# The x chunks of a state-space layer: hi part of the weights times both parts of the tokens in one 512-column matmul

## The reference

```
h = rmsnorm(x, norm_g) * (1 + scale) + shift
q, k, v, z_a, xbc, z_s, dt_f, dt_b, g_a, g_s = split_cols(h @ w_in, IN_SPLITS)
xbc = jax.nn.silu(centred_conv(xbc, conv_w, conv_b))        # 5 taps along the tokens
xs, b_ssm, c_ssm = split_cols(xbc, (SSD_WIDTH, BC_WIDTH, BC_WIDTH))
y_f, s_f = ssd_scan(x4, dtf, a_f, bm, cm, s0_f)             # and one backward
y = y_f + jnp.flip(y_b, 1) + d_skip[:, None] * x4
y = y.reshape(bsz, length, SSD_WIDTH) * jax.nn.silu(z_s)
```

## Time and profile before

| | us |
|---|---|
| median of 3 runs | 2763.86 |
| lowest, highest | 2763.12, 2764.31 |
| span of the profiled execution | 2761.4 |
| TensorE busy | 2711.6 (98%) |
| VectorE busy | 1965.3 (71%) |
| ScalarE busy | 1481.9 (54%) |
| GpSimd busy | 172.1 (6%) |

### The profile page before, as it was taken

How to read it: one execution, slowest core, us unless ns; L and a number is a source line. 1 busy time by engine, 2 the same in 40 slices (tenths; PEclk the granted TensorE clock), 3 DMA queues, 4 the chain that set the end, 5 groups by cost and what they waited for, 6 DMA issues and landing times.

```text
span 2761.4 us, 39482 instructions
## 1 busy us (share of the span) xinstructions
PE 2711.6 (98%) x15824; PEld 2326.7 (84%) x15824; DVE 1965.3 (71%) x2292; ACT 1481.9 (54%) x2145; POOL 172.1 (6%) x242
## 2 busy tenths in 40 slices
...
DMA packets 175670, 627.89 MB, mean 227 GB/s; under 512 B 21028, under 2 KB 23332, under 8 KB 175104
## 3 DMA queue, kind: packets, MB, share of 16 engines
...
...
## 4 chain that ended last, share of the span: by engine, by line
PE 88%; DVE 6%; DMA 2%; ACT 2%; issue 1%; SPq 0%; DVEq 0%; POOLq 0%; POOL 0%; ACTq 0%
PE PM L490 19%; PE PM L502 19%; PE PM L491 19%; PE PM L506 7%; PE PM L495 7%; PE PM L496 7%; PE A L785 6%; DMA Zt<-in_w_mod 2%; DVE w_l L468 1%; DVE arena L567 1%; DVE X L1589 1%; PE PM L782 1%; PE A L782 1%; ACT w_h L463 1%; DMA raw<-in_w_in 1%
## 5 line engine op out<-in xcount | busy, mean ns | idle before, releaser
L468 DVE TENSOR_TENSOR w_l<-raw,w_h 128x1024 fp32r<-128x1024 f32 (+1 forms) x880 | 1058.7, 1220 | 671.3 <-ACT w_h L463 663.8
L463 ACT ACTIVATE w_h<-raw 128x1024 fp32r<-128x1024 f32 (+1 forms) x880 | 905.0, 1046 | 796.0 <-PE PM L502 558.4
L490 PE MATMUL PM<-w_h,hT_h 128*128 128x512 f32 x1408 | 563.5, 400 | 2.1 <-issue 1.8
L491 PE MATMUL PM<-w_h,hT_l 128*128 128x512 f32 x1408 | 549.2, 390 | 0.0
L495 PE MATMUL PM<-hT_h,w_h 128*128 128x256 f32 x1920 | 479.1, 287 | 3.2 <-DVE X L1589 1.7
L496 PE MATMUL PM<-hT_l,w_h 128*128 128x256 f32 x1920 | 470.3, 283 | 0.0
L490 PE MATMUL PM<-w_h,Z 128*128 128x512 f32 x1016 | 399.2, 393 | 0.9 <-issue 0.9
L491 PE MATMUL PM<-w_h,Z 128*128 128x512 f32 x1016 | 395.7, 389 | 0.0
L502 PE MATMUL PM<-w_l,hT_h 128*128 128x512 f32 x1408 | 377.3, 390 | 0.0
L495 PEld LDWEIGHTS PM<-hT_h,w_h 128*128 128x128 f32 x1920 | 367.2, 191 | 11.3 <-issue 6.9
L496 PEld LDWEIGHTS PM<-hT_l,w_h 128*128 128x128 f32 x1920 | 367.8, 192 | 2.1 <-issue 1.4
...
## 6 DMA issues: line engine op xcount, KB each, us to landing
...
raw<-in_w_ps SPq DMA_DIRECT2D x128, 512.0 KB, 4.7
...
```

The lines of the kernel that those rows point to most:

```text
L463: act.activation(w_h[:, k % RING, :, 0:n], half_raw(k, n), ACT.Copy).then_inc(hi_ready, 1)
L468: dve.tensor_tensor(w_l[:, k % RING, :, 0:n], half_raw(k, n), w_h[:, k % RING, :, 0:n].bitcast(F32), ALU.subtract).then_inc(lo_ready, 1)
L490: pe.matmul(tok_out(s), hi[:, kt, tk], wh, start=kt == 0, stop=False, skip_group_check=True)
L491: pe.matmul(tok_out(s), lo[:, kt, tk], wh, start=False, stop=False, skip_group_check=True)
```

## The change

For groups 1 to 7 of each layer the x chunk is computed in another form; group 0 and all other chunks stay.

- hT_h and hT_l become the two planes of one tensor hT. A matmul with a w_h tile streams hT[:, :, kt], 512 columns: the sum from the high part of the tokens lands in the left half of a PSUM bank, the one from the low part in the right half. w_l still meets the high part only, 256 columns, into the left half. A half then has 8 matmuls of 512 columns and 8 of 256.
- The sums take twice the PSUM. So w_in of these chunks is laid out by quarters (four contraction slices of 256 channels in one 512 KB piece): halves 0 to 3 make channel tiles 0 and 1 in the banks used before, halves 4 to 7 make tiles 2 and 3 in A[:, 2:4].
- ScalarE copies the right halves to SBUF (`copy_low`, steps 6 and 10), VectorE adds the left halves (`sum_x`, steps 6 and 9). The sum, x_sum, is in SBUF (Zt[:, 6]).
- The centre tap (`center_x`, steps 8 and 11, two instructions each) and the taps (`conv_x`, steps 10 and 12, eight each) read x_sum from SBUF instead of PSUM.
- The first bank pair is free once `sum_x(g, 0)` has read it. `x_wide` waits before half 4 for `stores` of the group before, `final_states` for `sum_x`.
- To stay within the number of semaphores, a few of the prologue's are merged.

```diff
+        def mm_wide(pe, c, i, banks):
+            k = K(c, i)
+            w = [t[:, k % RING].rearrange("p t n -> p (t n)") for t in (w_h, w_l)]
+            pe.wait_ge(hi_ready, k + 1)
+            for kk in range(4):
+                kt = 4 * (i % 4) + kk
+                for t in range(2):
+                    at = kk * 256 + t * P
+                    pe.matmul(banks[:, t, :].rearrange("p (x n) -> p x n", x=2), w[0][:, at:at + P], hT[:, :, kt],
+                              start=kt == 0, stop=False, skip_group_check=True)
+            pe.wait_ge(lo_ready, k + 1)
+            for kk in range(4):
+                kt = 4 * (i % 4) + kk
+                for t in range(2):
+                    at = kk * 256 + t * P
+                    mm = pe.matmul(banks[:, t, 0:256], w[1][:, at:at + P], hT_h[:, kt], start=False, stop=kt == KT - 1,
+                                   skip_group_check=True)
+            mm.then_inc(w_used, 1)
...
+                def copy_low(g, part):
+                    chunk_done(act, base + PH_SSD + g * 2, 4 + 4 * part)
+                    if part == 0:
+                        act.wait_ge(s_("conv_done"), L * 12 + 4 + g)
+                    banks = A[:, 2:4, :] if part else pair(0)
+                    act.activation(x_sum[:, part * 512:(part + 1) * 512]..., banks[:, :, 256:512], F.Copy).then_inc(s_("x_low_copied"), 1)
...
+                    if g:
+                        st[6] = st.get(6, []) + [lambda: copy_low(g, 0)]
+                        st[8] = st.get(8, []) + [lambda: center_x(g, 0)]
+                        st[10] = st.get(10, []) + [lambda: copy_low(g, 1)]
+                        st[11] = [lambda: center_x(g, 1)] + st.get(11, [])
...
+                def sum_x(g, part):
+                    dve.wait_ge(s_("x_low_copied"), 2 * (L * (NG - 1) + g - 1) + part + 1)
+                    banks = A[:, 2:4, :] if part else pair(0)
+                    held = x_sum[:, part * 512:(part + 1) * 512].rearrange("p (t n) -> p t n", t=2)
+                    ins = tt(held, banks[:, :, 0:256], held, ALU.add)
...
+                def conv_x(g, part):
+                    for j in (0, 1, 3, 4):
...
+                            o_ = x_tile(xc, t)[:, :, lo_:hi_]
+                            ins = dve.scalar_tensor_tensor(out=o_, in0=x_tile(x_sum, t)[:, :, lo_ + d:hi_ + d], scalar=taps(j, 4 * g + t),
+                                                           in1=o_, op0=ALU.mult, op1=ALU.add)
...
-                    st[12] = [lambda: conv_1(g)] + st.get(12, [])
-                    st[13] = [lambda: conv_2(g)] + st.get(13, [])
+                    if g:
+                        st[6] = st.get(6, []) + [lambda: sum_x(g, 0)]
+                        st[9] = st.get(9, []) + [lambda: sum_x(g, 1)]
+                        st[10] = st.get(10, []) + [lambda: conv_x(g, 0)]
+                        st[12] = [lambda: conv_x(g, 1)] + st.get(12, [])
```

More of the change, by code:

```diff
@@ L188 @@
 Z_RUN, Z_LOAD = z_tiles()
+WIDE_BLOCKS = [B_XBC + g for g in range(1, NG)]
 def raw_order():
@@ L258, in halves, with quarters @@
         return w.reshape(depth, rows // 256, 2, P, cols // N, N).transpose(0, 4, 1, 3, 2, 5).reshape(depth, cols // N, rows // 256, P, 2 * N)
+    def quarters(w):
+        depth, rows, cols = w.shape
+        return w.reshape(depth, 4, 4, P, cols // N, 2, N // 2).transpose(0, 4, 5, 1, 3, 2, 6).reshape(depth, cols // N, 8, P, 2 * N)
     given = {k: np.asarray(v) for k, v in inputs.items()}
     w_in, w_mod = given["w_in"], given["w_mod"]
-    given["w_in"] = halves(np.concatenate([w_in[:, :, :C_DT], w_in[:, :, C_GA:]], axis=2))
+    columns = np.concatenate([w_in[:, :, :C_DT], w_in[:, :, C_GA:]], axis=2)
+    given["w_in"], by_quarter = halves(columns), quarters(columns)
+    for b in WIDE_BLOCKS:
+        given["w_in"][:, b] = by_quarter[:, b]
     given["w_dt"] = w_in[:, :, C_DT:C_GA].reshape(DEPTH, 1, D_MODEL // 256, 2, P, 2 * NH).transpose(0, 1, 2, 4, 3, 5)\
@@ L324, in build @@
         decay_rows = [Zt[:, 7, :], Zt[:, 15, :]]
+        x_sum = Zt[:, 6, :]
         def CB(q):
@@ L662, in psum_sub, with x_tile @@
             return banks[:, t // 2, (t % 2) * 256:(t % 2 + 1) * 256].rearrange("p (s n) -> p s n", s=2)
+        def x_tile(held, t):
+            return held[:, t * 256:(t + 1) * 256].rearrange("p (s n) -> p s n", s=2)
         def x_banks(q):
@@ L791, in _ @@
             pe.wait_ge(s_("mod_rows_loaded"), 4 * DMA)
-            transpose(A[:, 1, 0:96], rows[0:96, 3]).then_inc(s_("mod_rows_T"), 1)
+            transpose(A[:, 1, 0:96], rows[0:96, 3]).then_inc(s_("c_T"), 1)
             end_phase(pe)
@@ L960, in final_states @@
                         pe.wait_ge(s_("st_stored"), L * NG + q)
+                    if q < NG - 1:
+                        pe.wait_ge(s_("x_summed"), L * (NG - 1) + q + 1)
                     pe.wait_ge(s_("xw_ready"), L * NG + q + 1)
@@ L980, in ssd_steps, with x_wide @@
                     return st
+                def x_wide(g, steps):
+                    c = base + PH_SSD + g * 2
+                    bank_wait(pe, 0, ub + U_SSD + g)
+                    for i in range(8):
+                        if i == 4 and g > 1:
+                            pe.wait_ge(s_("st_stored"), L * NG + g - 1)
+                        mm_wide(pe, c, i, pair(0) if i < 4 else A[:, 2:4, :])
+                        tiles_behind(K(c, i))
+                        for step in steps.get(i, ()):
+                            step()
                 def ssd_body(g, steps):
-                    halves(base + PH_SSD + g * 2, "ch", 0, ub + U_SSD + g, hT_h, hT_l, steps)
+                    if g:
+                        x_wide(g, steps)
+                    else:
+                        halves(base + PH_SSD, "ch", 0, ub + U_SSD, hT_h, hT_l, steps)
                     halves(base + PH_SSD + g * 2 + 1, "tok", 1, ub + U_SSD + g, hT_h, hT_l, steps, first=8)
```

66 lines of the change are left out of this document (49 added, 17 removed).

## The result

| | median, us | from to | runs |
|---|---|---|---|
| before | 2763.49 | 2762.69 to 2764.31 | 4 |
| changed | 2815.47 | 2813.73 to 2816.71 | 4 |

The changed kernel is slower: ratio 1.0188, 95% interval 1.0176 to 1.0200. The forecast was 2816. The profiled execution has a span of 2813.4 us, 52.0 more than before.

A forecast was written before the change was run, and what follows sets the result against it. A ScalarE-VectorE loop of 53.1 us, covered by TensorE's 53.7, was to become the bound at 57.7: +47.9 us for twelve groups and +4.4 for group 1, together +52, giving 2816 us, range 2802 to 2828.

The forecast's parts named there:

- the slack: ScalarE's wait for TensorE at the third exp: TensorE's 53.7 us covers the 53.1 us loop by 0.6 us.
- TensorE's waits: Per group after the change, TensorE waits 1.4 us for the fourth M and some 3.4 for step 13's w_l.
- group 1's 1.24 us: Lead of group 2's first w_h, taken off group 1's growth: 4.1 - 0.64 - 1.24 = +2.2 us in each layer.
- TensorE no longer holds up the exp: Third exp on ScalarE: its wait for TensorE goes once the loop is the longer, -0.59 us per group.
- pause behind conv_2: VectorE's pause between the end of the taps and the next w_l goes: -0.15 us per group.
- GpSimd: Taps with two SBUF tensors alternate with GpSimd's four instructions, +3.4 us; step 13's w_l gets 0.75 back: +2.65 per group.
- period: Time of each of groups 2 to 7: 53.70 us before, 57.7 after, +4.0 for 12 groups in two layers.
- The loop: ScalarE from step 0's w_h to step 9, then VectorE to add_y: 53.1 us round, sets group time once longer than TensorE's.
- rival 2: Loop from step 0's w_h to add_y has unseen slack, TensorE sets all: -12.0 us, 2752, faster; chance 0.07.
- Rival 3: VectorE keeps the port, GpSimd starves; add_y and final_states wait 2 to 3 us: 2800 to 2815; chance 0.74 together with forecast.
- TensorE's gain: Wide halves take 0.107 us less matmul time each: 0.86 us per group, 12.0 us over 112 halves at most.

The follow-up runs named there:

- e5: Kernel before with four more ScalarE centre instructions behind step 8's w_h of groups 1 to 7, written to an unread place: 2777.4 us, ratio 1.0052.
- e9: Changed kernel with eight useless 512-column matmuls filling TensorE's wait in step 13 of groups 1 to 7: 2806.6 us, ratio 1.0161 to the kernel before.
- e1: Changed kernel with the sums of x left in PSUM, where center_x and the taps read them: 2773.3 us, ratio 1.0035 to the kernel before.
- e7: Changed kernel with sums in PSUM, center_x(g, 0) behind step 9 and squares behind the next group's second w_h: 2753.3 us, ratio 0.9962 to the kernel before.
- e4: Kernel before with three more ScalarE copies of 128x256 behind step 8's w_h of groups 1 to 7, written to an unread place: 2764.1 us, ratio 1.0004.
- e2: Changed kernel with GpSimd's four instructions of a group cut to 4 of every 64 columns: 2765.0 us, ratio 1.0007 to the kernel before.
- e6: Changed kernel with a group's squares moved behind the next group's second w_h on ScalarE: 2807.3 us, ratio 1.0157 to the kernel before.
- e11: Changed kernel with the taps of conv_x(g, 1) on VectorE ahead of the fourth M instead of behind it: 2811.5 us, ratio 1.0177 to the kernel before.

## Why the prediction came out

The direction, the size and the mechanism were right; the slack, TensorE's waits and the place of group 1's 1.24 us were not, and their errors cancelled in the total. Per group of 2 to 7:

| term | forecast | measured | from |
|---|---|---|---|
| TensorE no longer holds up the exp | -0.59 | -1.01 + 0.39 = -0.62 | e5, e9 |
| copy_low(g, 0) | +0.48 | +0.48 | profile after |
| center_x(g, 0) | +1.00 | +0.98 | profile after |
| sum_x(g, 1) | +0.60 | +0.61 | profile after |
| pause behind conv_2 | -0.15 | -0.15 | profile after |
| GpSimd | +2.65 | 3.17 - 0.74 = +2.43 | profile after, e1 |
| period | 57.7 | 57.43 by the sum, 57.38 seen | |

- **The loop** is real: 52.69 us before (e5), and 52.69 + 0.48 + 0.98 + 0.61 - 0.15 + 2.43 = 57.04 for the changed kernel, where e9, which takes TensorE's clock out, shows 56.98. e7, where the loop is cut down, gives the forecast's rival 2: TensorE sets all.
- **The slack** was read wrongly. I took the idle time in front of one instruction of one group, 0.59, for the slack of a loop. It was 1.01; e4 paid nothing for 0.92. Six of the twelve groups show 0.80 to 0.82 at the same instruction, group 6 had spent 0.20 on a transfer before it, and the usual overlap of 0.10 was missing too: 0.91 of the 1.01 stood in the trace of before. e2 supports the 52.69: with GpSimd out of the way the same sum gives 52.69 + 0.48 + 0.98 + 0.61 - 0.15 - 0.74 = 53.87, and its period is 53.83.
- **TensorE's waits** were the step that failed. I gave its spare 4.85 us to the fourth M (1.4) and to step 13's w_l (3.4). It waits 2.45 to 2.84 for w_l and hardly ever for M. Part of this is a size: at full clock (e9) the two are 2.85 and 0.47. The other part is a step that the forecast lacks: behind 11 of the 14 waits the granted clock fell to 0.50, TensorE lost 1.6 to 2 us there (e6, and the busy time of group 6), and with them the wait for M. The earlier trace rows show a clock of 1.00 and no idle time, but the trace of before has such a fall, between the layers, and the forecast makes no use of it (the matmuls behind a wait, then a stretch in the columns of the earlier trace rows):

```profile
1415.24 1.31 PE L782 MATMUL PM<-cst,arena 128*128 128x128 f32 x8 [1.93 <-DVE arena L1633]
```
```profile
1415.98:1419.39 3.41, 3.41 (x25) 1.81 (x24) 2.79 (x10) 0.12 (x1) 0.00 (x0) 0.50 1.02 318
```

  It costs the changed kernel about 6 us (e9).
- **Luck.** In a period at half clock, the missing 0.42 of slack and the 0.39 that the clock gives back have about one size. In the total, the twelve periods grew by 44.3 us and not by 47.9. Of the 44.3, 2.1 lie in the two groups with a wait of ScalarE for a transfer and some 2.6 are the clock's (e9); without these the sum would have been 8 us too high. I had written that the transfers cost nothing, as nothing waits there. In return group 1 and the body behind group 7 grew by 7.4 and not by 4.4. That 2816 met 2815.5 is the sum of these.
- **GpSimd**: each instruction cost 0.79 instead of 0.85, and step 13's w_l got its 0.74 back as foretold. By the rule of the Trainium skill ("SBUF — State Buffer", Who interferes with whom), a VectorE instruction with two SBUF inputs contends with a GpSimd instruction that reads SBUF; e1 (one input to PSUM) and e2 (GpSimd made short) agree, and e11 shows it for w_l. By the fixed parts that the Trainium skill gives ("VectorE: DVE Perf Modes", The TRN2 errata) taps would be dearer from PSUM; the runs do not agree, eight taps take 3.14 from SBUF and 3.11 from PSUM (e1).
- **Rival 3** (GpSimd starves): no. Its four take 5.3 us instead of 4.75, shorter than the 5.5 to 6 of the forecast, and nobody waits for them.
- **TensorE's gain** of 0.86 a group is 0.67 (e7), none of which shows in the changed kernel.
- **Group 1** grew by 3.2 in each layer instead of 2.2. The clock has no part in it, e9 shows the same 59.6 us. The chain from the third exp on got 0.98 + 0.61 - 0.15 + 2.43 = 3.87 longer (foretold 4.1), and in the first layer that exp came 27.93 us behind the first w_h instead of 28.47, 0.54 earlier (foretold 0.64): 3.3. But the 1.24 us of lead that I took off there is TensorE's, and the pace of the next groups is ScalarE's: it comes back only behind group 7. At full clock it does, 51.5 us in e9 against 52.6 before, so that both together are +2.1 per layer, near the foretold 2.2. In the changed kernel the half clock behind group 7's wait takes it and more: 53.1.
